# Attention in a two-block model: value products for two query tiles at a time, and scores over all keys as two products of 264 columns

## The reference

```python
scale = MLA_QK ** -0.5
blocks = [(0, N_META)] + [(s, min(s + ATTN_BLOCK, L)) for s in range(N_META, L, ATTN_BLOCK)]
outs = []
for s, e in blocks:
    sc = jnp.einsum('bqhd,bkhd->bhqk', q[:, s:e], k[:, :e]).astype(jnp.float32) * scale
    mask = jnp.arange(e)[None, :] <= jnp.arange(s, e)[:, None]
    p = jax.nn.softmax(jnp.where(mask, sc, -jnp.inf), axis=-1).astype(v.dtype)
    outs.append(jnp.einsum('bhqk,bkhd->bqhd', p, v[:, :e]))
o = jnp.concatenate(outs, axis=1).reshape(bsz, L, MLA_HEADS * MLA_V)
```

## Time and profile before

| | |
|---|---|
| median of 3 runs | 2567.28 us |
| lowest and highest | 2566.45, 2567.41 us |
| the profiled execution | 2567.46 us |
| its span in the trace | 2565.6 us |
| mean granted TensorE clock | 0.997 |
| DVE, ACT, POOL busy | 44%, 39%, 45% |

### The profile page before, as it was taken

One profiled execution on the slowest core, in us unless ns is written; L12 is line 12 of the kernel. 1 busy time (PEld: TensorE's weight loads), 2 busy tenths in 40 slices (PEclk: granted clock), 3 DMA queues, 4 the chain that ended last, 5 costly groups with the idle time before them and its releaser, 6 DMA issues.

```text
span 2565.6 us, 37415 instructions
## 1 busy us (share of the span) xinstructions
PE 2520.2 (98%) x15184; PEld 2177.6 (85%) x15184; DVE 1134.9 (44%) x1696; ACT 988.9 (39%) x1540; POOL 1167.2 (45%) x1513
## 2 busy tenths in 40 slices
PE   8999999999999999899999899999999999999999
PEld 6888888778888887899999899999997777788887
DVE  6444452165445422778888532111125554411211
ACT  4433333343333333444444433222235564422321
POOL 5455445445544544344444355444435011655553
PEclk9999999999999999999999999999999999999999
DMA  4333333223333332222212133223222000333332
GB/s 149 93 108 110 95 101 100 87 79 106 110 95 100 104 97 66 66 62 63 75 59 67 57 92 99 83 91 93 89 77 82 18 24 20 104 98 95 96 92 90
DMA packets 63579, 217.72 MB, mean 85 GB/s; under 512 B 8432, under 2 KB 10864, under 8 KB 63408
## 3 DMA queue, kind: packets, MB, share of 16 engines
q1 hardware_dynamic: 57248, 202.05, 26.1%
q10 hardware_dynamic: 6160, 13.28, 1.6%
HBM read 213.20 MB, written 2.10 MB: 84 GB/s over the span
## 4 chain that ended last, share of the span: by engine, by line
PE 92%; DVE 5%; ACT 1%; issue 1%; POOL 1%; DMA 0%; ACTq 0%; DVEq 0%
PE psum L408 80%; PE psum L1071 1%; PE psum L506 1%; PE psum L524 1%; POOL sb_w_lo L381 1%; PE psum L695 1%; PE psum L726 1%; PE psum L1039 1%; PE psum L1037 1%; PE psum L420 1%; PE psum L1056 1%; PE psum L1016 0%; DVE sb_xdt L2141 0%; PE psum L959 0%; DVE sb_xdte L2141 0%
## 5 line engine op out<-in xcount | busy, mean ns | idle before, releaser
L381 POOL TENSOR_TENSOR sb_w_lo<-sb_w_raw,sb_w_hi 128x256 fp32r<-128x256 f32 x1508 | 1166.1, 805 | 1375.5 <-ACT sb_w_hi L1203 1375.3
L408 PE MATMUL psum<-sb_h_hi,sb_w_hi 128*128 128x512 f32 (+1 forms) x2648 | 808.6, 347 | 26.2 <-POOL sb_w_lo L381 14.5
L408 PE MATMUL psum<-sb_h_lo,sb_w_hi 128*128 128x512 f32 (+1 forms) x2648 | 790.5, 340 | 0.0
L408 PE MATMUL psum<-sb_h_hi,sb_w_lo 128*128 128x512 f32 (+1 forms) x2648 | 787.8, 339 | 0.0
L1203 ACT ACTIVATE sb_w_hi<-sb_w_raw 128x1024 fp32r<-128x1024 f32 x377 | 395.8, 1055 | 520.2 <-PE psum L408 294.2
L408 PEld LDWEIGHTS psum<-sb_h_hi,sb_w_hi 128*128 128x128 f32 x2648 | 455.8, 189 | 92.6 <-issue 22.9
L408 PEld LDWEIGHTS psum<-sb_h_lo,sb_w_hi 128*128 128x128 f32 x2648 | 454.8, 189 | 57.4 <-issue 3.8
L408 PEld LDWEIGHTS psum<-sb_h_hi,sb_w_lo 128*128 128x128 f32 x2648 | 454.7, 189 | 55.7
L408 PE MATMUL psum<-sb_mix_hi,sb_w_hi 128*128 128x264 f32 (+1 forms) x1424 | 414.3, 336 | 8.0 <-POOL sb_w_lo L381 4.2
L408 PE MATMUL psum<-sb_mix_lo,sb_w_hi 128*128 128x264 f32 (+1 forms) x1424 | 410.0, 334 | 0.0
L408 PE MATMUL psum<-sb_mix_hi,sb_w_lo 128*128 128x264 f32 (+1 forms) x1424 | 408.7, 333 | 0.0
(11 more groups left out here) (299 smaller groups left out, 2339.4 us busy)
## 6 DMA issues: line engine op xcount, KB each, us to landing
sb_w_raw<-in_weights SPq DMA_DIRECT2D x377, 512.0 KB, 3.5
sb_decay<-in_decay ACTq DMA_DIRECT2D x16, 640.0 KB, 3.7
sb_resid<-in_x SPq DMA_DIRECT2D x4, 512.0 KB, 9.2
sb_s<-in_decay ACTq DMA_DIRECT2D x16, 128.0 KB, 3.8
out<-sb_resid SPq DMA_DIRECT2D x8, 256.0 KB, 2.1
sb_s<-in_positions ACTq DMA_DIRECT2D x1, 256.0 KB, 7.2
sb_cols<-in_cols ACTq DMA_DIRECT2D x1, 158.5 KB, 4.5
sb_table<-in_rope_table ACTq DMA_DIRECT2D x1, 132.0 KB, 3.6
```

What stands on the lines that cost most here:

```text
L381: low = e.tensor_tensor(g.w_lo[:, u % 4, at], g.w_raw[:, u % 2, at], g.w_hi[:, u % 4, at].bitcast(F32), ALU.subtract)
L408: mm = e.matmul(g.psum[0:m, at + b, 0:wd], w[:, slot, P * i:P * i + m], xs[:, tile, c:c + wd], start=first and n == 0, stop=last and n == 2)
```

## The change

It does two things, both on TensorE alone. The value products of two query tiles now stand together: tiles 0 and 1 in step 6, tiles 3 and 2 in step 1 of the next pair. The scores of tile 3 stand at columns 248 to 511 of bank 4 and 0 to 263 of bank 5, and are made by two products of 264 columns instead of one of 16 and one of 512. At the end of the attention, tile 3 and tile 2 of the last pair stay apart.

```diff
--- before.py
+++ after.py
@@ -147,8 +147,8 @@
 
 QT = SEQ // P
 KEYS = [META + P * (t + 1) for t in range(QT)]
-STEPS = ((0, 0, 4 * 512), (1, 0, 5 * 512), (0, 3, 4 * 512 + 496), (0, 1, 5 * 512),
-         (1, 1, 4 * 512), (0, 2, 5 * 512), (1, 3, 4 * 512 + 496), (1, 2, 5 * 512))
+STEPS = ((0, 0, 4 * 512), (1, 0, 5 * 512), (0, 3, 4 * 512 + 248), (0, 1, 5 * 512),
+         (1, 1, 4 * 512), (0, 2, 5 * 512), (1, 3, 4 * 512 + 248), (1, 2, 5 * 512))
 NS = len(STEPS)
 ALL_STEPS = PAIRS * NS
 
@@ -163,7 +163,8 @@
 Q_BLOCKS = ((), (), (), (0,), (1, 2), (3,), (4,), (5,))
 
 
-V_TILES = {(0, 5): (0, 0, 1), (0, 6): (1, 3, 4), (1, 0): (3, 2, 6), (1, 1): (2, 5, 7)}
+V_TILES = {(0, 6): (0, 1), (1, 1): (3, 2)}
+V_STEPS = {0: (0, 1), 1: (3, 4), 3: (2, 6), 2: (5, 7)}
 
 
 QK_HALF = HALF + 4
@@ -1033,8 +1034,8 @@
         e.wait_ge(S[done], step // 4 + 1 if done == "pt_meta" else step + 1)
     q, k = g.q2[:, pair % 2, h, P * t:P * t + P], g.k2[:, pair % 2, h, :]
     if t == QT - 1:
-        e.matmul(g.flat(at, META), q, k[:, 0:META], start=True, stop=True)
-        e.matmul(g.flat(at + META, SEQ), q, k[:, META:L], start=True, stop=False)
+        e.matmul(g.flat(at, HALF), q, k[:, 0:HALF], start=True, stop=True)
+        e.matmul(g.flat(at + HALF, HALF), q, k[:, HALF:L], start=True, stop=False)
     else:
         e.matmul(g.flat(at, KEYS[t]), q, k[:, 0:KEYS[t]], start=True, stop=False)
     e.matmul(g.flat(at + KEYS[t] - P, P), g.ident16[:, :], g.mask[:, :], start=False,
@@ -1058,10 +1059,10 @@
     e.transpose(to, p[:, 0:P], g.ident[:, :]).then_inc(S["p_turned"], 1)
 
 
-def pe_times_v(g, e, pair, after, n):
-
-    S = g.S
-    t, first, second = V_TILES[after, n]
+def pe_times_v(g, e, pair, t):
+
+    S = g.S
+    first, second = V_STEPS[t]
     e.wait_ge(S["pt"], NS * pair + second + 1)
     if t == 0 and pair:
         e.wait_ge(S["out2"], pair)
@@ -1146,10 +1147,11 @@
         pe_scores(g, e, i)
         if i >= 1:
             pe_turn_p(g, e, i - 1)
-        if (0, n) in V_TILES:
-            pe_times_v(g, e, pair, 0, n)
-        if pair and (1, n) in V_TILES:
-            pe_times_v(g, e, pair - 1, 1, n)
+        for t in V_TILES.get((0, n), ()):
+            pe_times_v(g, e, pair, t)
+        if pair:
+            for t in V_TILES.get((1, n), ()):
+                pe_times_v(g, e, pair - 1, t)
         if more and n == 0:
             pe_pair_block(g, e, pair + 1, 6)
             pe_pair_block(g, e, pair + 1, 7)
@@ -1166,10 +1168,10 @@
                 m, k = FILL[i, at]
                 pe_mla_out(g, e, m, [k])
     pe_turn_p(g, e, ALL_STEPS - 1)
-    pe_times_v(g, e, PAIRS - 1, 1, 0)
+    pe_times_v(g, e, PAIRS - 1, 3)
     pe_mla_out(g, e, 3, range(0, 2))
     pe_share_turn(g, e, PAIRS - 1)
-    pe_times_v(g, e, PAIRS - 1, 1, 1)
+    pe_times_v(g, e, PAIRS - 1, 2)
     pe_mla_out(g, e, 3, range(2, 5))
     for m in range(3):
         pe_mla_out(g, e, m, range(7, 8))
```

## The result

The changed kernel takes 2570.95 us (median of 15 runs, 2569.41 to 2573.42), the kernel before 2565.29 us in 15 runs (2564.53 to 2567.95; the three of the table of times before are among them). The ratio is 1.0020 with a 95% interval of 1.0013 to 1.0027: about 5.7 us slower, clear of no change, and at the line of 0.2% that the prediction drew.

What follows compares the result with a forecast made beforehand. The attention was taken as a ring of TensorE, VectorE and ScalarE, where moved cover becomes waiting. Terms 4.02, -0.04 - 0.20, 0.98 and -0.26 gave +4.5 us on 2567.46, less 0.18 for the median: 2571.8 us, range 2567.0 to 2574.4.

Steps and rivals of the forecast that it cites:

- Steps 0 to 2: Tile 3's products move to step 1; transposes of step 0 wait for ScalarE's copy: 0.67 us later, six pairs.
- released by PE's own work: Behind step 2's scores, norm sums and later scores were said to follow TensorE's own work, carrying the 0.67 us on.
- The price of a group: Value products in the attention: 0.16 us fixed for each group, besides 0.054 us for each product.
- rival 2: TensorE is the bound all the way, step 0's transposes finding the copy ready: faster, 2561.7 us; chance 0.08.
- The split: Tile 3's scores as two products of 264 columns take 0.98 us, saving 0.20 us a step on 16 steps.
- Steps 5 to 7: Tile 0's products move to step 6; removing them ahead of step 6's scores gains nothing: 0.14 us later a pair.
- Second pair: Its copy ends earlier, so steps 0 to 2 give -0.04 us in place of +0.67; steps 5 to 7 give +0.14.
- Last pair: Steps 0 to 2 as in earlier pairs, +0.67 us; steps 5 to 7 without a wait, -0.26 in place of +0.14.
- Rival 3: No net change: VectorE's maximum of step 0 comes about 0.7 us earlier, so 2567.8 us; chance 0.15.
- rival 4: The clock falls to 1.2 GHz behind TensorE's idle time in step 0: 19 us more, 2591 us; chance 0.07.
- rival 5: A larger loss: the 264-column products save nothing, +2.8 us, so 2574.6 us and up; chance 0.10.
- a fixed part of 0.16 us for each tile in a group: Range term: if both tiles in a group keep a fixed part, 15 groups of two tiles add up to 2.4 us.

Runs made afterwards that it cites:

- runs 5 to 7: Changed kernel with ScalarE's copy of step 7's transposes earlier (5), VectorE's low part later (6), both (7): 2568.46, 2566.35, 2563.86 us.
- Run 1: Kernel before with only tile 3's scores as two products of 264 columns, value products unmoved: 2565.19 us, ratio 0.9993.
- run 11: Kernel before with the 264-column scores, and step 0's transposes copied by VectorE instead of ScalarE: 2563.91 us, ratio 0.9986.
- Run 3: Changed kernel with tiles 3 and 2 apart again in steps 0 and 1, tiles 0 and 1 still grouped: 2568.49 us, ratio 1.0005.
- Run 12: Changed kernel with early copy and later low part, tiles 0 and 1 apart, and the last pair's tiles 3 and 2 apart: 2561.68 us, ratio 0.9981.
- run 7: Changed kernel with both ScalarE's early copy and VectorE's later low part: 2563.86 us, ratio 0.9997.
- run 8: Changed kernel with ScalarE's early copy, VectorE's later low part, and tiles 0 and 1 apart again: 2561.41 us, ratio 0.9986.
- Run 6: Changed kernel with VectorE's low part made behind step 0's maximum instead of ahead, for pairs 0 to 4: 2566.35 us, ratio 1.0004.

## Why the prediction was right, and where its steps were off

The sum was +4.5 us; +5.7 was measured by the medians, and 5.3 in the trace (5.20 + 0.12). The mechanism is the one forecast: cover that became waiting. That 2570.95 us lies only 0.9 under the 2571.8 of the forecast is luck in part: the loss was 1.2 us larger than the sum, but the kernel before came out at 2565.29 us in 15 runs, 2.0 under the three on which the forecast stood.

In the trace, the 0.8 us that the sum lacks are these: first pair 0.18, second 0.09, third to seventh 0.33 together, last 0.22.

*Steps 0 to 2, forecast +0.67 us in six pairs: 0.71.* From step 0's scores to step 3's it is 10.57 us (2048.14 to 2058.71) where it was 9.86 (2048.28 to 2058.14). The cover that becomes waiting is confirmed by runs 5 to 7. Two small terms in it were off and nearly cancel. A copy on ScalarE releases TensorE 0.15 us after its end (2052.23 to 2052.38), not 0.05 as an exponential does: +0.10. And the prediction had the norm sums behind step 2's scores "released by PE's own work". They were waiting for ScalarE's keys; with the loss ahead of them they no longer do, and from the mask of step 2 to step 3's scores it is 2.88 us (2055.83 to 2058.71) where it was 2.94 (2055.20 to 2058.14).

*The price of a group, 0.16 us besides its products: too small.* It counts from the group's first start on and leaves out what a group costs ahead of that. Without tile 3's 20 rows step 1's scores come 1.44 us earlier (4.03 to 2.59), not 1.24, so the group itself is worth 1.44 - 20 x 0.054 = 0.36. That is why 1.41 us lie between mask and transposes and not 1.2, and why TensorE waits 0.79 us ahead of step 6's scores and not 0.6. The sum didn't suffer, since both places end in a wait for another engine; rival 2, whose gain of 15 groups is made of this price, has it too small.

*The split, forecast 0.20 us a step on 16 steps: the price right (0.19), its arrival only in part.* In the changed kernel step 2's saving counts in full from the second pair on, because the grouping has made TensorE late for everything else. In the first pair nothing of that sort stands ahead of step 2, and its saving is lost: the pair was forecast at -0.06 and came out at +0.12 (20.60 against 20.48 us). Run 1 shows the loss for every pair, and run 11 what took it: with the copy out of the way its first pair is 20.01 us, against 20.26 in run 1.

*Steps 5 to 7, forecast +0.14: 0.17,* that is 24.23 - 23.35 less the 0.71. The removed products gave nothing in step 5, as forecast. Run 3 against run 1 puts the grouping at 0.33 where the sum has 0.43 - 0.09 = 0.34.

*Second pair, forecast +0.10 in all: 0.19* (23.52 against 23.33 us). The copy's release, 0.15 us after its end in place of 0.05, accounts for it (ScalarE's copy ends at 2003.78, the transposes start at 2003.93).

*Last pair, forecast +0.41: 0.63* (30.66 against 30.03 us, from its first scores to the last value products). Here a step failed: steps 0 to 2 of the last pair were taken as in the pairs before it, with a wait for ScalarE's copy. In step 0 no projection of another pair stands there, but the output projection, and it waited 1.3 us for VectorE's low part; for the copy nothing waited. Run 12 shows it.

*Rivals.* TensorE as the bound all the way (rival 2) needed the copy by the time TensorE comes; run 7 all but makes that true. Its stretch is 1.73 us under the kernel before, not 5.6: the rival named the right condition for step 0, but step 6's scores wait for an exponential as well, and there grouping costs 0.34 us a pair (run 8). Rival 3 had VectorE's maximum of step 0 come 0.7 us earlier, at a price of 4.0 us. Nothing of it was seen: that maximum starts 2.47 us behind the step's scores (2048.14 to 2050.61), before it was 2.46 (2048.28 to 2050.74). Run 6 makes its condition true: the maximum starts 1.74 us behind (2045.75 to 2047.49), and the stretch is 3.64 us shorter than in the changed kernel. No change of the clock followed waits of 0.8 and 1.2 us (rival 4): it stayed at 1.00. The products of 264 columns saved what they should, so the larger loss of rival 5 didn't come. In the forecast's own range stood a fixed part of 0.16 us for each tile in a group; 36 products in 2.12 us are against it. (The upper end that follows from it is 2571.8 + 2.4 = 2574.2, not 2574.4.)

## What to carry to other kernels

Where engines go round in a ring, a piece of work on the busiest engine has two values: its length, and the time that it covers. Before moving it, write down beside each wait of the later place who releases it and what stands ahead of that release in the other engines' orders; those orders are often the cheaper thing to change. And a busy share of 98% with 1.6 us of waits in 170 doesn't mean that a saving arrives: look at which start follows which end by 0.05 to 0.15 us, since this can be a release that comes only just in time, and a saving ahead of it is lost until that release comes earlier too.

## What the runs showed of the hardware

A narrow float32 product costs more than its columns. Two passes of 16 columns and two of 512 took 1.18 us, four passes of 264 columns 0.99, for the same 528 columns. The difference is the same where TensorE doesn't wait ahead of them, in step 2 of the last pair: 1.08 us (2148.21 to 2149.29) and 0.89 (2152.68 to 2153.57), where the 528 columns by themselves come to 0.88. That the weights' load is the reason is the prediction's argument; no run takes it apart from the rest.

Value products of 64 output rows, two heads in turn, run at 0.054 us each, and 36 in a row took 2.12 us where the formula from groups of 12 and 20 gives 2.10. From a group's first start to the next work 0.16 us come on top; with what it costs ahead of its start, one group less is worth 0.36 us. The Trainium skill, TensorEngine Tiling (Array Packing), Key Properties, says that changing the tiling mode drains TensorE. A price for each group, whatever its length, agrees with it; no run shows that the drain is the whole of it.

A copy out of PSUM on ScalarE releases TensorE 0.15 us after its end, an exponential with the read of its sum 0.05 to 0.06 us.

The granted clock at the start of the attention (1980 to 2001 us) was 0.84 in one execution and 1.00 in thirteen, with the same code ahead of it. Why is open.
